# A fused hybrid layer on one core: inputs laid out before the launch, x transposed in memory, its squares summed by VectorE

## The chip, the cores and the metric

One core of a Trainium2 chip runs the whole program. The metric is the device time of one execution in microseconds (us). It has a TensorE (PE) for matrix products, a VectorE (DVE), a ScalarE (ACT), a GpSimd engine (POOL) and a SyncE (SP), whose queue only starts transfers here; 16 DMA engines move data between device memory and the on-chip memory SBUF. TensorE writes its results to PSUM.

## What is computed

One decoder layer over 256 tokens of 2048 features, in float32. The input is normalised, multiplied by one wide matrix, mixed by three groups of heads (retention, gated DeltaNet, block attention), gated, and multiplied by an output matrix:

```python
def rms_norm(x, w):
    return x * lax.rsqrt(jnp.mean(x * x, axis=-1, keepdims=True) + 1e-6) * w

def hybrid_layer(x, norm_w, w_in, ...):
    h = rms_norm(x, norm_w)
    proj = jnp.einsum('btd,de->bte', h, w_in)        # 256 x 2048 by 2048 x 8204
    # 4 retention heads, 6 DeltaNet heads (convolution, L2 norm, gates ga and gb,
    # triangular solve per chunk), 6 attention heads; each times SiLU of its gate
    y = jnp.concatenate([y_ret, y_gdn, y_moba], axis=-1)
    return x + jnp.einsum('bte,ed->btd', y, w_out)   # 256 x 2048 by 2048 x 2048
```

## The kernel before, in words

The instructions of each engine are written out by hand, each engine with its own program, and semaphores order them. The two projections are cut into 160 weight tiles of 128 x 1024 numbers. Tile n is loaded in two transfers of 256 KB into one of 8 buffers `w_raw` (`load`, L396); ScalarE rounds it to a shorter format, `w_hi` (`high_part`, L485, one of 4 buffers); VectorE takes the rest, `w_lo` (`low_part`, L366); TensorE multiplies with both. The activations are split the same way into `hT[:, k, 0]` (high) and `hT[:, k, 1]` (low), for 16 feature blocks k. A tile is used up when TensorE has run its 8 "units", each one 512-column product with `w_hi` and one 256-column product with `w_lo`. The positions of all other work are counted in units: `advance(u)` on ScalarE and VectorE emits the high and low parts that are due before unit u, and `stream(u)` on TensorE emits units up to u. A tile's low part is emitted 2.5 tiles ahead of its use (`LEAD`, `LOW_AT`).

The first group of products (tiles 0 to 7, units 0 to 63) makes the first four columns of blocks of the DeltaNet heads, and the program is special there. x arrives by rows (`x_sb`, tokens on the partitions) in five pieces (`load_piece`). TensorE transposes each pair of feature blocks into PSUM (`x_block`, L1598, by `all_x_blocks`), a tile or two ahead of their use. ScalarE multiplies by the norm's weight and rounds to the high part (`x_high`), VectorE makes the low part from the same PSUM block (L1048), and GpSimd adds both to a whole float32 block (`whole`, L871), which the small products for the gates need (`ab_products`, L1686). The norm's weights come by rows too and are transposed by TensorE (L1649), the other parameters likewise (L1695). The squares of x are summed per token from the rows, half by ScalarE (L557), half by VectorE (L1034).

The scale 1/rms of each token does not go into hT but is applied afterwards: GpSimd raises the mean square to the power -0.5 (`power`), TensorE spreads it over all partitions (L1679), VectorE copies it to `rb` (L1065), and the first projections are multiplied by `rb` (L1074, L1076). From there on VectorE's program is: two additions and two products for the first two sections (L1072, L1074), the gate rows (L1076), then the convolutions of the heads (L1092) and the gates' short chain, with a low part L369 between them whenever one is due.

SyncE's queue issues x's pieces and the weight tiles in one order; from tile 8 on it waits for the low part of tile n - 8.

Of the kernel before, what the change touches and what calls it, by code (L numbers as in the profile page):

```python
# [19 lines left out]
F32 = mybir.dt.float32  # L20
F32R = mybir.dt.float32r
ALU = mybir.AluOpType
# [3 lines left out]
P = 128  # L26
# [35 lines left out]
LOW_AT = 4  # L62

# [11 lines left out]
K_DECAY = K_LEVEL + (LEVELS - 3) * QUART  # L75
K_DIST = K_DECAY + RET * P
K_FIRST_T = K_DIST + 3 * P
K_STACK = K_FIRST_T + QUART
K_KDEC = K_STACK + QUART
K_QDEC = K_KDEC + RET  # L80
K_SUM = K_QDEC + RET
K_COLS = K_SUM + 2 * GDN

# [7 lines left out]
R_ROWS = R_K + 1  # L91

# [43 lines left out]
def layer(nc, x, norm_w, w_in, conv_w, a_log, dt_bias, ret_norm_w, gdn_norm_w, q_norm_w, k_norm_w, w_out,  # L136
          table, out):
    ctx = ExitStack()
    with ctx:
# [12 lines left out]
        bias = sb("bias", [P, 2, GDN])  # L152
        sb("pad", [P, QUART // 2])
# [8 lines left out]
        prow = sb("prow", [R_ROWS, P])  # L162
        pcol = sb("pcol", [P, R_ROWS])
# [33 lines left out]
        x_sb = big[:, :].rearrange("p (c n) -> p c n", c=C)  # L197

        abT = vT[:, 0, :]
        junk_a, junk_v = kq[:, :].rearrange("p h c k t -> p (h c k t)"), sq[:, :].rearrange("p h c k t -> p (h c k t)")  # L200
        def first_bank(k):

            return (mx[0], mx[2], mx[1], mx[3])[k] if k < 4 else mx[k // 2 % 4]
# [66 lines left out]
        def section(g, s):  # L270

            return g % 3, s % 2, 2 * (g // 3) + s // 2

# [17 lines left out]

        def tile_at(n):

            if n < HEADS * TPH:
                return n // TPH, n % TPH
            g, q = OUT_TILES[n - HEADS * TPH]
            return HEADS + g, q
# [67 lines left out]

        def low_part(eng, n):  # L366
# [9 lines left out]
        X_PIECES = [(0, 2), (2, 4), (4, 8), (8, 12), (12, 16)]  # L376
        X_LANDED = [16 * C] + [16] * (len(X_PIECES) - 1)
        SQUARES_AT = {3: 1, 4: 2, 5: 3}

        def load_piece(eng, i):  # L380

            piece = slice(X_PIECES[i][0] * P, X_PIECES[i][1] * P)
            if i:
                eng.dma_start(x_sb[:, :, piece], x[0, :, piece].rearrange("(c p) n -> p c n", p=P)).then_inc(S(f"x_in{i}"), 16)
                return
            for c in range(C):
                eng.dma_start(x_sb[:, c, piece], x[0, c * P:(c + 1) * P, piece]).then_inc(S(f"x_in{i}"), 16)
# [5 lines left out]
        def _(sp):  # L393
            load_piece(sp, 0)

            def load(n):  # L396
                group, q = tile_at(n)
                rows = slice(q * TK * P, (q + 1) * TK * P)
                if n >= NRAW:
                    wait_lo(sp, n - NRAW)  # L400
                dst = w_raw[:, n % NRAW, :].rearrange("p (k n) -> p k n", k=TK)
                if group < HEADS:
                    kind, j = PAIRS[group // 2]
                    heads = {"gdn": GDN, "ret": RET, "moba": MOBA}[kind]
                    first_col = {"gdn": GDN_COL, "ret": RET_COL, "moba": MOBA_COL}[kind]
                    h = 2 * j + group % 2
                    if group == 0:
                        done = [S(f"w_first{n}"), S(f"w_in{n}")] if n < 2 else [S(f"w_in{n % NRAW}")] * TK
                        src = w_in[0, rows, GDN_COL:GDN_COL + 2 * GDN * P].rearrange("(k p) (i c) -> p k i c", p=P, i=2)[:, :, :, 0:2 * P]
                        dst = dst.rearrange("p k (i c) -> p k i c", i=2)  # L410
                        for k in range(TK):
# [1548 lines left out]
```

## Time and profile before

| | us |
|---|---|
| median of 3 runs (510.35 to 510.66) | 510.56 |
| the profiled execution | 510.59 |
| its span, first to last instruction | 508.8 |
| TensorE busy | 503.6 (99%) |
| VectorE busy | 338.8 (67%) |
| ScalarE busy | 279.0 (55%) |
| GpSimd busy | 169.8 (33%) |

The profiled execution took 1.8 us more than its span. TensorE is busy through nearly all of the span. The other engines' shares are means over the program; VectorE's is far above its mean in the first 80 us. Each matmul's end is modelled, so a busy TensorE may still hold a short wait; the weight loads (PEld) show such waits better.

### The profile page before, as it was taken

Reading aid. Unit: us, or ns where it says so; the run is one execution under the profiler, and the core shown is the slowest. Engines: PE = TensorE matmul, PEld = TensorE weight load, DVE = VectorE, ACT = ScalarE, POOL = GpSimd, SP = SyncE. Lnnn points to the kernel's source line nnn. Section 1 sums busy time; section 2 is a strip of 40 time slices with the busy share of each in tenths; the row PEclk is TensorE's granted clock in tenths of the full one; section 3 lists DMA queues with packets and bytes.
Section 4 is the critical chain, followed back from the end, with each engine's and each line's share of the span. In section 5 each row is a group of like instructions: output and inputs, shape, how many; then the busy total and the mean of one; then the engine's idle time right before and its main releaser. Section 6 shows DMA issues by size and latency. Waiting matters only on the chain.

```text
span 508.8 us, 8943 instructions
## 1 busy us (share of the span) xinstructions
PE 503.6 (99%) x3442; PEld 424.1 (83%) x3442; DVE 338.8 (67%) x506; ACT 279.0 (55%) x464; POOL 169.8 (33%) x230
## 2 busy tenths in 40 slices
PE   8999999999999999999999999999999999999997
PEld 6888888888888888888888888888888888888885
DVE  5989998889766876564467455755567566646551
ACT  5776756764347676564537354664556456344340
POOL 5763245445122312134054115506050614230000
PEclk9999999999999999999999999999999999999999
DMA  8997666565654556473975676777775557757711
GB/s 280 346 323 200 166 162 169 159 174 144 190 132 122 132 158 158 134 197 69 292 196 145 167 222 164 201 196 190 193 187 168 166 172 232 221 185 222 260 43 41
DMA packets 154988, 92.61 MB, mean 182 GB/s; under 512 B 15971, under 2 KB 143938, under 8 KB 154946
## 3 DMA queue, kind: packets, MB, share of 16 engines
q1 hardware_dynamic: 151456, 89.86, 62.8%
q10 hardware_dynamic: 3490, 2.18, 1.5%
q8 instruction: 27, 0.44, 0.3%
q14 instruction: 15, 0.12, 0.1%
HBM read 89.00 MB, written 2.10 MB: 179 GB/s over the span
## 4 chain that ended last, share of the span: by engine, by line
PE 99%; POOL 0%; DVE 0%; DVEq 0%; issue 0%; POOLq 0%
PE pj L1574 20%; PE pj L1577 20%; PE pj L1576 20%; PE pj L1552 14%; PE pj L1553 7%; PE pj L1630 3%; PE pj L1639 2%; PE mx L1734 1%; PE pj L1549 1%; PE mx L1787 1%; PE mx L1769 1%; PE mx L1601 1%; PE pj L1647 1%; PE mx L1845 1%; PE mx L1907 1%; PE pj L1548 1%
## 5 line engine op out<-in xcount | busy, mean ns | idle before, releaser
L369 DVE TENSOR_TENSOR w_lo<-w_raw,w_hi 128x1024 fp32r<-128x1024 f32 x160 | 200.7, 1262 | 78.2 <-ACT w_hi L489 77.3
L489 ACT ACTIVATE w_hi<-w_raw 128x1024 fp32r<-128x1024 f32 x158 | 166.1, 1057 | 121.0 <-PE pj L1577 103.7
L1574 PE MATMUL pj<-w_hi,hT 128*128 128x512 f32 x320 | 126.5, 395 | 0.0
L1576 PE MATMUL pj<-w_hi,hT 128*128 128x512 f32 x320 | 126.1, 394 | 0.0
L1577 PE MATMUL pj<-w_lo,hT 128*128 128x512 f32 x320 | 124.7, 390 | 0.0
L1552 PE MATMUL pj<-hT,w_hi 128*128 128x512 f32 x300 | 109.0, 403 | 0.0
L1553 PE MATMUL pj<-hT,w_lo 128*128 128x256 f32 x300 | 84.1, 280 | 0.0
L1577 PEld LDWEIGHTS pj<-w_lo,hT 128*128 128x128 f32 x320 | 60.1, 188 | 12.2
L1574 PEld LDWEIGHTS pj<-w_hi,hT 128*128 128x128 f32 x320 | 60.1, 188 | 12.1
L1576 PEld LDWEIGHTS pj<-w_hi,hT 128*128 128x128 f32 x320 | 60.2, 188 | 11.5
L1552 PEld LDWEIGHTS pj<-hT,w_hi 128*128 128x128 f32 x300 | 56.3, 188 | 13.2 <-DVE w_lo L369 0.6
L927 POOL COPY mT<-mT 32x128 f32<-32x128 f32 x80 | 40.5, 506 | 60.1 <-issue 45.7
L1553 PEld LDWEIGHTS pj<-hT,w_lo 128*128 128x128 f32 x300 | 56.6, 189 | 0.7
L858 POOL TENSOR_TENSOR sm<-sm,cst 128x4 f32<-128x4 f32 (+2 forms) x12 | 15.8, 1314 | 111.8 <-DVE sm L1417 39.3
L1574 PE MATMUL pj<-w_hi,yT 128*128 128x512 f32 x128 | 50.3, 393 | 0.0
L1577 PE MATMUL pj<-w_lo,yT 128*128 128x512 f32 x128 | 49.8, 389 | 0.0
L1576 PE MATMUL pj<-w_hi,yT 128*128 128x512 f32 x128 | 49.8, 389 | 0.0
L897 POOL TENSOR_TENSOR ev<-ev 128x256 f32<-128x256 f32 x22 | 23.7, 1078 | 67.2 <-ACT ev L504 67.0
L1092 DVE SCALAR_TENSOR_TENSOR big<-raw,pcol,big 128x256 f32<-128x256 f32 x54 | 33.8, 627 | 3.2 <-ACT big L527 1.9
L927 POOL COPY kq<-mT 32x128 f32<-32x128 f32 x56 | 32.0, 572 | 11.2 <-DVE mT L1380 8.0
L1577 PEld LDWEIGHTS pj<-w_lo,yT 128*128 128x128 f32 x128 | 24.0, 188 | 5.0
L1576 PEld LDWEIGHTS pj<-w_hi,yT 128*128 128x128 f32 x128 | 24.0, 188 | 4.9
(239 smaller groups left out, 541.2 us busy)
## 6 DMA issues: line engine op xcount, KB each, us to landing
w_raw<-in_w_in_dram SPq DMA_DIRECT2D x256, 256.0 KB, 3.4
w_raw<-in_w_out_dram SPq DMA_DIRECT2D x64, 256.0 KB, 4.1
big<-in_x_dram SPq DMA_DIRECT2D x9, 256.0 KB, 5.3
out_dram<-sq ACTq DMA_DIRECT2D x7, 256.0 KB, 5.8
big<-in_x_dram SPq DMA_DIRECT2D x3, 512.0 KB, 7.1
cst<-table_dram SPq DMA_DIRECT2D x1, 682.0 KB, 9.3
kq<-vr SPq DMA_DIRECT2D x32, 16.0 KB, 1.8
kq<-mT SPq DMA_DIRECT2D x24, 16.0 KB, 1.9
```

The lines of the kernel that those rows point to most:

```text
L369: eng.tensor_tensor(w_lo[:, n % NSPLIT, :], w_raw[:, n % NRAW, :], w_hi[:, n % NSPLIT, :].bitcast(F32), ALU.subtract).then_inc(S("lo"), 1)
L489: act.activation(w_hi[:, n % NSPLIT, :], w_raw[:, n % NRAW, :], ACT.Copy).then_inc(S("hi_done"), 1)
L858: return pool.tensor_tensor(sm[:, dst:dst + n], sm[:, src:src + n], cst[:, K_POW:K_POW + n], ALU.pow)
L897: pool.tensor_tensor(ev[:, n % 2, 0:T], ev[:, n % 2, 0:T], ev[:, n % 2, T:2 * T], ALU.add).then_inc(S("halves"), 1)
L927: ins = pool.tensor_copy(dst[i:i + QUART, :, a:a + QUART], src[a:a + QUART, :, i:i + QUART])
L1092: ins = dve.scalar_tensor_tensor(dst, raw_of(j, h, i, slice(k, k + T)), tap, dst, ALU.mult, ALU.add)
L1552: pe.matmul(pj[s][:, :], high, hT[:, kc].rearrange("p a t -> p (a t)"), start=first, stop=False)
L1553: ins = pe.matmul(pj[s][:, 0:T], low, hT[:, kc, 0, :], start=False, stop=False)
L1574: ins = pe.matmul(bank[:, :], src[:, kc, 0, tok], hi[:, k, :], start=first, stop=False)
L1576: pe.matmul(bank[:, :], src[:, kc, 1, tok], hi[:, k, :], start=False, stop=False)
L1577: ins = pe.matmul(bank[:, :], src[:, kc, 0, tok], lo[:, k, :], start=False, stop=last)
L1630: pe.matmul(pj[s][:, cols], block_of(hi, 0, s, k), hT[:, TK * t + k].rearrange("p a t -> p (a t)")[:, cols], start=t == 0 and a == 0, stop ...
```

## The change

The host part of the program now passes the same numbers in another layout, and the kernel reads these:

- x transposed, feature-major, with the 16 columns of the norm's weight in front. It lands in the place of the whole blocks (`home`), in six pieces; `whole_pair` names two neighbouring blocks. (x by rows is still an input for the sum at the end.)
- the weights cut into the 160 tiles, each 128 x 1024 contiguous: one transfer of 512 KB for each, two of 256 KB for the first three (`HALVED`). All parameters as columns (`cols`); the gates' weights apart.
- `x_high` and `x_low` read x from SBUF. All 32 transposes of x and the two of parameters are gone, and so are the four filling ones (`keep_busy`) and GpSimd's 16 additions.
- GpSimd multiplies the gates' weights by the norm's weight, once.
- Squares: ScalarE squares 8 pairs of blocks (128 x 512) into `big`, VectorE adds the eight (`add_squares`) and the two halves of the sum (`total_squares`), and TensorE sums over the partitions with two one-column products in the middle of tile 7. The power and the spreading over partitions now follow the gates' products.
- In tiles 0 to 2 the high and low products alternate by half tile, and VectorE makes the low part in halves.

```diff
+        def x_squared(b):
+            return big[:, b * 2 * T:(b + 1) * 2 * T]
+        def half_low_part(eng, n, k):
+            cols = slice(k * 512, (k + 1) * 512)
+            eng.wait_ge(S(("hi_first", "hi_done")[k]), n + 1)
+            eng.tensor_tensor(w_lo[:, n, cols], w_raw[:, n, cols], w_hi[:, n, cols].bitcast(F32), ALU.subtract)...
-        X_PIECES = [(0, 2), (2, 4), (4, 8), (8, 12), (12, 16)]
+        X_PIECES = [(0, 2), (2, 4), (4, 6), (6, 8), (8, 12), (12, 16)]
+        SQUARES_AT = {1: (0,), 2: (1,), 3: (2,), 4: (3, 4), 5: (5,), 6: (6,), 7: (7,)}
...
+                sp.dma_start(w_raw[:, n % NRAW, :], tiles[n]).then_inc(S(f"w_in{n % NRAW}"), 16)
...
+            def square(b):
+                act.activation(x_squared(b), whole_pair(b), ACT.Square).then_inc(S("squared"), 1)
             def x_high(k):
-                act.activation(hT[:, k, 0, :], first_bank(k)[:, k % 2 * T:(k % 2 + 1) * T], ACT.Copy,
-                               scale=pcol[:, R_NORM + k:R_NORM + k + 1]).then_inc(S("h_hi"), 1)
+                x_landed(act, k)
+                act.activation(hT[:, k, 0, :], whole(k), ACT.Copy, scale=norm_cols[:, k:k + 1])...
...
-            for n in range(KC):
-                pool.tensor_tensor(whole(n), hT[:, n, 0, :].bitcast(F32), hT[:, n, 1, :].bitcast(F32), ALU.add)...
+            pool.tensor_tensor(wab[:, :, 0:AB], wab_in, pcol[:, R_NORM:R_CONV].unsqueeze(2).broadcast_to([P, KC, AB]),
+                               ALU.mult).then_inc(S("pool_step"), 1)
+            pool.wait_ge(S("norm_step"), 10)
+            power(6, 10, 2).then_inc(S("pool_step"), 1)
...
+            def x_low(k):
+                dve.wait_ge(S("h_hi"), k if k else 1)
+                dve.scalar_tensor_tensor(hT[:, k, 1, :], whole(k), norm_cols[:, k:k + 1],
+                                         hT[:, k, 0, :].bitcast(F32), ALU.mult, ALU.subtract)...
+            def add_squares(b):
+                dve.wait_ge(S("squared"), b + 1)
+                dve.wait_ge(S("norm_step"), b)
+                dve.tensor_tensor(x_squared(0), x_squared(0), x_squared(b), ALU.add)...
...
+                x_low(2 * b)
+                x_low(2 * b + 1)
+                advance(UPT * (b - LEAD) + LOW_AT + 1)
+                add_squares(b - 2)
+            add_squares(6)
+            add_squares(7)
+            total_squares()
+            advance(UPT * (KC // 2 - LEAD) + LOW_AT + 1)
+            dve.wait_ge(S("norm_psum"), 1)
+            dve.tensor_scalar(sm[:, 10:12], mx[3][:, 0:C], 1.0 / D, EPS, ALU.mult, ALU.add)...
             dve.wait_ge(S("norm_psum"), 2)
             dve.tensor_copy(rb[:, :], mx[1][:, 0:T]).then_inc(S("rb_done"), 1)
...
+                first_group_high(t, range(TK))
                 if t == TPH - 1:
-                    pe.wait_ge(S("rstd_done"), 1)
+                    pe.wait_ge(S("norm_step"), 9)
                     for c in range(C):
-                        ins = pe.transpose(mx[1][:, c * P:(c + 1) * P], sm[:, 6 + c:7 + c].broadcast_to([P, P]), ident)
-                    ins.then_inc(S("rb_psum"), 1)
+                        ins = pe.matmul(mx[3][:, c:c + 1], x_squared(7)[:, c * P:(c + 1) * P], er[:, 0, 0:1], ...)
...
+            pe.wait_ge(S("pool_step"), 1)
             ab_products().then_inc(S("abt_psum"), 1)
+            pe.wait_ge(S("pool_step"), 2)
+            for c in range(C):
+                ins = pe.transpose(mx[1][:, c * P:(c + 1) * P], sm[:, 6 + c:7 + c].broadcast_to([P, P]), ident)
+            ins.then_inc(S("norm_psum"), 1)
```

On TensorE, the end of the first group before (L1601 transposes x, L1630 and L1639 are high and low products, L1679 spreads 1/rms, L1695 transposes parameters, L1690 is the gates):

```order
L1630 MATMUL pj<-hT,w_hi 128x512 x8
L1639 MATMUL pj<-hT,w_lo 128x256 x8
L1601 MATMUL mx<-cst,big 128x128 x4
L1630 MATMUL pj<-hT,w_hi 128x512 x8
L1639 MATMUL pj<-hT,w_lo 128x256 x8
L1630 MATMUL pj<-hT,w_hi 128x512 x8
L1679 MATMUL mx<-cst,sm 128x128 x2
L1639 MATMUL pj<-hT,w_lo 128x256 x8
L1695 MATMUL mx<-cst,prow 128x95
L1690 MATMUL mx<-home,wab 32x256 x16
L1552 MATMUL pj<-hT,w_hi 128x512
```

and now (L1629 and L1642 are high and low products, L1661 sums the squares, L1670 is the gates, L1678 spreads 1/rms):

```order
L1629 MATMUL pj<-hT,w_hi 128x512 x8
L1642 MATMUL pj<-hT,w_lo 128x256 x8
L1629 MATMUL pj<-hT,w_hi 128x512 x8
L1642 MATMUL pj<-hT,w_lo 128x256 x8
L1629 MATMUL pj<-hT,w_hi 128x512 x8
L1661 MATMUL mx<-er,big 128x1 x2
L1642 MATMUL pj<-hT,w_lo 128x256 x8
L1670 MATMUL mx<-home,wab 32x256 x16
L1678 MATMUL mx<-cst,sm 128x128 x2
L1563 MATMUL pj<-hT,w_hi 128x512
```

The transposes are gone, the sum of squares stands where the spreading stood, and the spreading has moved behind the gates' products.

On VectorE, the same place before (L1048 low part of x, L369 low part of a tile, L1061 and L1063 finish the sum of squares, L1065 copies `rb`, L1068 copies parameters, L1072 and L1074 scale the first sections, L1076 the gates):

```order
L1048 SCALAR_TENSOR_TENSOR hT<-mx,pcol,hT 128x256 x2
L369 TENSOR_TENSOR w_lo<-w_raw,w_hi 128x1024
L1061 TENSOR_REDUCE sm<-sm 128x2
L1063 TENSOR_SCALAR sm<-sm 128x2
L1048 SCALAR_TENSOR_TENSOR hT<-mx,pcol,hT 128x256 x2
L369 TENSOR_TENSOR w_lo<-w_raw,w_hi 128x1024
L1065 COPY rb<-mx 128x256
L369 TENSOR_TENSOR w_lo<-w_raw,w_hi 128x1024
L1068 COPY pcol<-mx 128x79
L1072 TENSOR_TENSOR ev<-ev 128x256
L1074 TENSOR_TENSOR raw<-ev,rb 128x256
```

and now (L1039 low part of x, L418 low part of a tile, L1051 adds squares, L1045 the two halves, L1076 takes the mean, L1079 copies `rb`, L1083 and L1085 scale the first sections):

```order
L1039 SCALAR_TENSOR_TENSOR hT<-home,hT 128x256 x2
L418 TENSOR_TENSOR w_lo<-w_raw,w_hi 128x1024
L1051 TENSOR_TENSOR big<-big 128x512 x3
L1045 TENSOR_TENSOR big<-big 128x256
L418 TENSOR_TENSOR w_lo<-w_raw,w_hi 128x1024
L1076 TENSOR_SCALAR sm<-mx 128x2
L1079 COPY rb<-mx 128x256
L1083 TENSOR_TENSOR ev<-ev 128x256
L1085 TENSOR_TENSOR raw<-ev,rb 128x256
```

The low part of tile 8 now stands ahead of the copy of `rb` instead of behind it, and three additions of squares end the first group.

## Rows read from the trace of the kernel before

**Rows 1.** The chain of waits, 0 to 62 us: start us, us, what.
```profile
4.45 0.68 PE mx L1601 x4
...
5.67 2.37 PE pj L1630 x12
...
24.76 0.96 PE pj L1639 x8
25.72 0.44 PE mx L1601 x4
26.16 1.85 PE pj L1630 x8
...
30.80 0.22 PE mx L1679 x2
...
32.05 1.86 PE mx L1690 x32
...
36.59 0.35 PE mx L1705 x4
```

**Rows 2.** Waits of the weight loads, whole span: total us, times, longest us.
```profile
PEld pj L1552 <- DVE w_lo L369: 0.6, 2, 0.3
```

**Rows 3.** Busy time in one stretch, VectorE alone, then clock, DMA share, GB/s.
```profile
31.00:57.60 26.60, 25.86 (x46) 1.00 0.81 226
```

**Rows 4.** Timeline, 31 to 58 us: start us, us, instructions.
```profile
31.05 0.42 DVE L1065 COPY rb<-mx 128x256 f32<-128x256 f32 x1 [1.66 <-PE mx L1679]
31.39 1.22 DVE L369 TENSOR_TENSOR w_lo<-w_raw,w_hi 128x1024 fp32r<-128x1024 f32 x1
32.53 0.23 DVE L1068 COPY pcol<-mx 128x79 f32<-128x79 f32 x1
32.68 0.41 DVE L1072 TENSOR_TENSOR ev<-ev 128x256 f32<-128x256 f32 x1
...
56.38 1.21 DVE L369 TENSOR_TENSOR w_lo<-w_raw,w_hi 128x1024 fp32r<-128x1024 f32 x1
...
57.65 0.19 PEld L1552 LDWEIGHTS pj<-hT,w_hi 128*128 128x128 f32 x1 [0.28 <-DVE w_lo L369]
```

**Rows 5.** Timeline, 4.8 to 5.4 us: start us, us, instructions.
```profile
4.80 0.63 ACT L495 ACTIVATE w_hi<-w_raw 128x512 fp32r<-128x512 f32 x1 [1.64 <-DMA w_raw<-in_w_in_dram]
```

**Rows 6.** Busy time of each engine in stretches, then clock, DMA share, GB/s.
```profile
2.00:3.00 1.00, 1.00 (x2) 0.34 (x1) 0.00 (x0) 0.99 (x2) 0.48 (x2) 1.00 0.82 241
3.00:4.00 1.00, 1.00 (x3) 0.34 (x1) 0.00 (x0) 0.16 (x1) 0.00 (x0) 1.00 1.00 306
...
5.00:10.00 5.00, 4.90 (x37) 4.27 (x36) 4.54 (x9) 4.06 (x9) 2.84 (x3) 1.00 1.02 333
10.00:15.00 5.00, 5.00 (x34) 4.34 (x32) 4.67 (x6) 3.56 (x7) 4.79 (x5) 1.00 1.08 390
```

**Rows 7.** Groups by shape, ScalarE: busy us, mean ns, idle before.
```profile
L489 ACT ACTIVATE w_hi<-w_raw 128x1024 fp32r<-128x1024 f32 x158 | 166.1, 1057 | 121.0 <-PE pj L1577 103.7 <-PE pj L1553 16.6
L557 ACT ACTIVATE kq<-big 128x512 f32<-128x512 f32 x4 | 2.5, 628 | 0.0
L781 ACT ACTIVATE yT<-mT,sm 128x256 fp32r<-128x256 f32 x4 | 1.8, 501 | 7.8 <-POOL mT L927 7.8
```

**Rows 8.** Single lines: duration ns min/median/max, first and last start.
```profile
L1048 DVE SCALAR_TENSOR_TENSOR hT<-mx,pcol,hT x16: 467/474/485, 5.6 to 27.8; 128x256 fp32r<-128x256 f32 x16
L1370 DVE SCALAR_TENSOR_TENSOR yT<-mT,sm,yT x4: 479/482/485, 268.0 to 314.7; 128x256 fp32r<-128x256 f32 x4
L1034 DVE SCALAR_TENSOR_TENSOR sq<-big x4: 1221/1222/1226, 8.0 to 23.3; 128x512 f32<-128x512 f32 x4
L369 DVE TENSOR_TENSOR w_lo<-w_raw,w_hi x160: 1183/1226/1767, 6.8 to 495.3; 128x1024 fp32r<-128x1024 f32 x160
L1015 DVE TENSOR_TENSOR sq<-pj,big x7: 681/684/692, 458.4 to 504.4; 128x512 f32<-128x512 f32 x7
L871 POOL TENSOR_TENSOR home<-hT x16: 736/1207/1819, 6.1 to 30.0; 128x256 f32<-128x256 f32 x16
```

More of the change, by code:

```diff
@@ L62 @@
 LOW_AT = 4
+HALVED = 3
 LEVELS = 7
@@ L133, in constants, with tile_at, section, weight_tiles @@
     return t.astype(np.float32)
-def layer(nc, x, norm_w, w_in, conv_w, a_log, dt_bias, ret_norm_w, gdn_norm_w, q_norm_w, k_norm_w, w_out,
-          table, out):
+def tile_at(n):
+    if n < HEADS * TPH:
+        return n // TPH, n % TPH
+    g, q = OUT_TILES[n - HEADS * TPH]
+    return HEADS + g, q
+def section(g, s):
+    return g % 3, s % 2, 2 * (g // 3) + s // 2
+def weight_tiles(w_in, w_out):
+    tiles = np.empty((TILES, P, TK * 512), np.float32)
+    for n in range(TILES):
+        group, q = tile_at(n)
+        rows = slice(q * TK * P, (q + 1) * TK * P)
+        if group >= HEADS:
+            g = group - HEADS
+            tile = w_out[0, rows, g * 512:(g + 1) * 512].reshape(TK, P, 512)
+        elif group == 0:
+            tile = w_in[0, rows, GDN_COL:GDN_COL + 2 * GDN * P].reshape(TK, P, 2, GDN * P)[:, :, :, 0:2 * P]
+        elif group < GDN:
+            p, h, i = section(group, q // 2)
+            at = GDN_COL + (i * GDN + 2 * p + h) * P
+            tile = w_in[0, q % 2 * UPT * P:(q % 2 + 1) * UPT * P, at:at + P].reshape(UPT, P, P)
+        else:
+            kind, j = PAIRS[group // 2]
+            heads, col = {"ret": (RET, RET_COL), "moba": (MOBA, MOBA_COL)}[kind]
+            h = 2 * j + group % 2
+            tile = w_in[0, rows, col:col + 4 * heads * P].reshape(TK, P, 4, heads * P)[:, :, :, h * P:(h + 1) * P]
+        tiles[n] = np.moveaxis(tile, 0, 1).reshape(P, TK * 512)
+    return tiles
+def columns(norm_w, conv_w, a_log, dt_bias, ret_norm_w, gdn_norm_w, q_norm_w, k_norm_w):
+    per_row = [a.reshape(-1, P).T for a in (norm_w, conv_w, ret_norm_w, gdn_norm_w, q_norm_w, k_norm_w)]
+    per_head = [np.broadcast_to(a.reshape(1, GDN), (P, GDN)) for a in (a_log, dt_bias)]
+    return np.ascontiguousarray(np.concatenate(per_row + per_head, axis=1))
+def layer(nc, x, turned_x, tiles, gate_w, cols, table, out):
     ctx = ExitStack()
@@ L393, in _ @@
         def _(sp):
-            load_piece(sp, 0)
             def load(n):
-                group, q = tile_at(n)
-                rows = slice(q * TK * P, (q + 1) * TK * P)
+                if n < HALVED:
+                    for k, done in enumerate((f"w_first{n}", f"w_in{n}")):
+                        if n == k == 1:
+                            load_piece(sp, 1)
+                        cols = slice(k * 512, (k + 1) * 512)
+                        sp.dma_start(w_raw[:, n, cols], tiles[n, :, cols]).then_inc(S(done), 16)
+                    return
@@ L594, in _ @@
                 else:
                     advance(UPT * (b - LEAD + 1))
-                if b in SQUARES_AT:
-                    square_sum(SQUARES_AT[b])
-                if b in (2, 3, 4, 5):
-                    load_params(b - 2)
+                for i in SQUARES_AT.get(b, ()):
+                    square(i)
             advance(64)
-            act.wait_ge(S("bias_in"), 2 * 16)
+            act.wait_ge(S("cols_in"), 16)
             act.activation(sm[:, 16:16 + GDN], bias[:, 0, :], ACT.Exp).then_inc(S("expa_done"), 1)
```

311 lines of the change are left out of this document (114 added, 197 removed).

## The prediction

> **What bounds the kernel now.** I read the page's busy times first (TensorE 99%), then the chain of waits, then who waits for whom, then VectorE's timeline. The chain is TensorE from end to end: in the first 62 us it goes without a gap from one product or transpose to the next [rows 1]. So an instruction that TensorE loses should shorten the program by its time. But the view of waits holds one short entry that says otherwise: twice a weight load waited for VectorE's low part, 0.3 us each [rows 2]. One of these is at 57.65 us, where tile 16 begins [rows 4]: L369 made that tile's low part from 56.38 to 57.59, and TensorE started right behind it. And VectorE has no room before that point: from 31.0 to 57.6 us it is busy 25.86 of 26.60 us, the rest being hops between instructions that depend on each other [rows 3]. That stretch begins at the copy of `rb` at 31.05 us, for which VectorE had waited 1.66 us [rows 4]. So there are two bounds: TensorE up to about 33 us, and VectorE's fixed row of instructions from the copy of `rb` to tile 16. What TensorE gains before 33 us is kept only as far as VectorE's row also begins earlier. After tile 16 TensorE is the bound again, and carries whatever shift it has there to the end.
>
> **The change on TensorE.** Seven batches of transposes of x behind the first product go, 0.44 us each in the chain [rows 1]: 3.1 us. The parameters' transpose (L1695) is about 0.1. Two one-column products come in; the nearest row is L1705, four records for two products, 0.35 us [rows 1], and I take 0.3. Start: the first product waits for the rounded half tile. It landed at 4.80 us [rows 5], issued behind two transfers of x; now behind one, and ScalarE makes one block of x ahead of it, so I expect the first product near 5.3 instead of 5.67: 0.4. Together 3.3 us, if nobody is late for it. Now who is late.
>
> **The change on VectorE and ScalarE, first group.** Low part of x: 0.474 us from PSUM; the same instruction with both tensors in SBUF is L1370, 0.482 [rows 8]: no change. Squares: before, four of 1.222 us; now seven additions of 128x512, 0.684 each by L1015, and one of 128x256, about 0.42 as L1065 or L1072 [rows 4, 8]. That is 4.9 before and 5.2 now: nothing gained, but they have moved: three additions and the halves now stand behind the last low part of x. GpSimd's 16 additions go. While they ran, L369 took up to 1.767 us against 1.183 at least [rows 8]; I take 1.22 for it in the first group. ScalarE: 0.50 for a high part of x from SBUF (L781), 1.06 for a tile, 0.63 for a square [rows 7]; that is 2.7 us per tile and less than TensorE's 0.96 + 1.85 = 2.81 [rows 1].
> Consecutive instructions on VectorE start 0.08 us closer than their duration (L369 starts at 31.39, takes 1.22, the next starts at 32.53 [rows 4]).
>
> VectorE's row, worked out. The data: up to the first half of tile 2, queues carry 2.16 MB (x's first 270 KB, parameters 55 KB, seven pieces of 262 KB). Before, the engines moved 241 GB/s in the third microsecond, 306 in the fourth, 333 from 5 to 10 us and 390 from 10 to 15 [rows 6]; with 2 KB rows instead of 1 KB I take 360. From 2.05 us on that gives 8.05; the first half tile landed 0.7 to 0.8 us later than the bytes ahead of it explain, so 8.85. ScalarE then rounds that half (0.6), squares a pair (0.55) and makes block 4 (0.5): 10.5 us. From there VectorE has left, by spacing: 12 low parts of x at 0.40 (4.8), 2 half tiles at 0.60 (1.2), 5 tiles at 1.13 (5.7), 5 additions at 0.60 (3.0), 2 that wait for the one before at 0.73 (1.5), and 0.45 for the halves: 16.7 us. I add 0.9 for ScalarE, which it follows closely in tiles 2 and 3, and 0.35 for the one time that GpSimd's product for the gates (192 columns; L871's 256 take 0.736 alone) runs into it. The squares are complete at 28.45 us.
>
> TensorE would be there at 27.1 (5.3, eight times 2.81 less the last low half of 0.95, and 0.3 of early waits), so it stands still 1.4 us in the middle of tile 7. Then: hop 0.1, sums 0.3, low half 0.95, gates 1.86, spreading 0.22 [rows 1]: 31.9 us. GpSimd's power is ready before that. TensorE's stream of units so starts at 31.9 instead of 33.9: 2 us earlier. VectorE copies `rb` (hop 0.05, 0.42 and 0.04 until the next may start) and begins L1072's successor at 32.4. Before, it began at 32.68 [rows 4], since the low part of tile 8 and the parameter copy stood between; these are gone from this place. The row behind it is the same, instruction by instruction, so tile 16's low part comes 0.25 us earlier than before, and TensorE, 2 us early at 33 us, gives 1.7 us of that back in waits at tiles 9, 14 and 16. No later wait in the views has less room, as the rest of both programs shifts alike.
>
> Sum: 510.59 (profiled execution, 0.03 above the median of the runs) less 0.25: **510.3 us**.
>
> Unknown costs, from both sides. Data rate in the first 10 us: 300 GB/s as before at its slowest, or 400; by the same steps VectorE's row begins 1.9 us later or 0.6 earlier than my 360 gives. An addition of squares in place: 0.684, or up to 0.73 each if it collides: +0.3. The collision with GpSimd: 0 to 0.6. The chain of low parts behind 33 us holds five pairs of GpSimd instructions that stretch VectorE's; they can fall luckier or worse by 0.5. Loads of 512 KB instead of two of 256: the buffers are 8 deep, ScalarE sat waiting for TensorE and not for data (L489: 103.7 us [rows 7]), so I cost it at nothing in the stream.
>
> The Trainium skill speaks against the low parts of x: "Vector Engine (DVE) Microarchitecture Reference", section "Points that are easy to get wrong", says that a scalar_tensor_tensor with two SBUF sources that are not bf16 runs at half throughput. The trace says both: L1034, which has two SBUF sources and also accumulates, takes 1.222 us for 512 columns; L1370, two SBUF sources and no accumulation, takes 0.482 for 256, the full rate. By the rows the rule does not hold without the accumulator; by the rule it would be rival 3.
>
> **The rivals.**
> 1. *VectorE does not hold it back.* If VectorE's row between 31 and 58 us is shorter now (fewer collisions with GpSimd, data at 400 GB/s and no collision before 28 us), TensorE keeps 1.2 to 2.3 us: 508.3 to 509.4. For it: the limit is a single point, tile 16, and only 0.3 us of waiting show it. Against: a stretch that is 97% busy in a fixed order.
> 2. *The data come late.* At 300 GB/s the half tile that I have at 8.85 lands at 10.0, and the later pieces add to it: the copy of `rb` ends at 34.1 and not 32.4, so VectorE is 1.5 us late at tile 16: 512.0. It decides from about 350 GB/s down (no gain), and is slower by 0.2% from 315 down. For it: 306 GB/s in the fourth microsecond with all DMA engines busy. Against: rows of 1 KB then, of 2 KB now.
> 3. *Low parts of x at half rate.* 0.69 us instead of 0.48, from L1034's 1.222 for 512 columns: 12 after the start of the full row, 2.5 us, less some 0.9 that now is waiting: 1.6 us later, 511.9. For it one kind of row, against it another.
> 4. *TensorE's sum works differently:* the two squares' sums wait longer than their row, 0.6 instead of 0.3, or VectorE's last four additions collide. That stays within 0.5 us of the forecast.
>
> **How the numbers follow.** 0.2% is 1.02 us; about what a measurement of this kernel can tell from no change. My forecast, VectorE takes the gain back, has 0.56 (with the fourth): of it 0.49 within 0.2%, 0.04 faster, 0.03 slower. Rival 1 has 0.22, nearly all faster. Rival 2 has 0.13 (0.10 slower), rival 3 0.07 (0.06 slower); 0.02 for what I have not seen. That makes faster 0.26, the same 0.53, slower 0.21. Range 508.8 to 512.1: it leaves out the better half of rival 1 and what lies beyond rivals 2 and 3; the forecast's own range is 509.6 to 511.2.
>
> **What the new profile would show.** Right: the first product near 5.3 us; TensorE idle 1 to 2 us inside tile 7, released by the addition L1045; VectorE idle before the copy L1079, released by the spreading; L1083 first at 32.0 to 32.8; waits of weight loads for L418 of 1.5 us or more in all between 33 and 58 us; L1039 at 0.48. Wrong: no such waits and a stream that stays 2 us early (rival 1); ScalarE waiting for transfers in tiles 2 to 5 (rival 2); L1039 at 0.69 (rival 3). If TensorE does not stop in tile 7, my row of VectorE is too long; if it stops for 3 us, too short.

## The result

| median us (lowest to highest) | before | changed |
|---|---|---|
| first timing | 510.48 (510.33 to 510.87, 8 runs) | 511.70 (511.38 to 512.81, 8 runs) |
| the profiled execution, span | 510.59, 508.8 | 511.47, 509.7 |

The ratio is 1.0024 (95% interval 1.0015 to 1.0034). The changed kernel is 1.2 us slower, where 510.3 was forecast; the time lies inside the range (508.8 to 512.1), but on the side that had 0.21, and above the forecast's own 509.6 to 511.2. Two later timings, each on one chip, gave ratios of 1.0030 (1.0020 to 1.0040) and 1.0021 (1.0012 to 1.0030).

The place where TensorE first waits for VectorE, from the timeline of the changed kernel (columns: start, duration, instructions, and in brackets the idle time before them with what ended it):

```profile
28.24 0.43 DVE L1045 TENSOR_TENSOR big<-big 128x256 f32<-128x256 f32 x1
28.58 1.22 DVE L418 TENSOR_TENSOR w_lo<-w_raw,w_hi 128x1024 fp32r<-128x1024 f32 x1
...
28.72 0.61 PE L1661 MATMUL mx<-er,big 128*128 128x1 f32 x4 [0.81 <-DVE big L1045]
29.16 1.01 PEld L1642 LDWEIGHTS pj<-hT,w_lo 128*128 128x128 f32 x8
...
29.72 0.15 DVE L1076 TENSOR_SCALAR sm<-mx 128x2 f32<-128x2 f32 x1
...
30.31 1.94 PE L1670 MATMUL mx<-home,wab 128*32 128x256 f32 x32
32.17 0.19 PEld L1678 LDWEIGHTS mx<-cst,sm 128*128 128x128 f32 x2 [0.41 <-issue]
32.17 0.43 PE L1678 MATMUL mx<-cst,sm 128*128 128x128 f32 x2
...
32.64 0.42 DVE L1079 COPY rb<-mx 128x256 f32<-128x256 f32 x1 [2.77 <-PE mx L1678]
...
33.10 0.43 DVE L1083 TENSOR_TENSOR ev<-ev 128x256 f32<-128x256 f32 x1
```

This answers to [rows 4]. The squares are complete at 28.67 us (28.24 + 0.43), and TensorE, idle for 0.81 us, goes on at once. The spreading L1678 comes last, so the copy of `rb` starts at 32.64, after VectorE has been idle for 2.77 us, and L1083 stands at 33.10, where its predecessor L1072 stood at 32.68 [rows 4]. The waits that follow, from the timeline of the weight loads at tiles 9, 14 and 16, and then the same wait in the view of waits (total, times, longest):

```profile
36.62 0.19 PEld L1563 LDWEIGHTS pj<-hT,w_hi 128*128 128x128 f32 x1 [0.71 <-DVE w_lo L418]
...
51.22 0.19 PEld L1563 LDWEIGHTS pj<-hT,w_hi 128*128 128x128 f32 x1 [0.62 <-DVE w_lo L418]
...
58.05 0.19 PEld L1563 LDWEIGHTS pj<-hT,w_hi 128*128 128x128 f32 x1 [0.58 <-DVE w_lo L418]
```
```profile
PEld pj L1563 <- DVE w_lo L418: 2.2, 4, 0.7
```

Before, the same wait summed to 0.6 us [rows 2]. Tile 16's first weight load stood at 57.65 [rows 4], now at 58.05. I set the first product of each unit against the same one of before (columns: start before; shift of the changed kernel, us):

```
unit 64 (stream begins)  33.85  -1.49
unit 72 (tile 9)         37.22  -0.59
unit 112 (tile 14)       51.21  +0.01
unit 128 (tile 16)       57.65  +0.41
unit 168                 75.09  +0.22
unit 304                130.54  +0.84
end of the projections'
last group, from        483.10  +0.99
```

So TensorE has 1.5 us in hand at the start of the stream and has lost 1.9 by tile 16. That is the forecast's mechanism with a larger loss: 1.7 was forecast. Of the 2.2 us in the view of waits 1.9 stand in these three waits. A second loss, which was not forecast, lies between units 296 and 304, in the triangular solve. The chain of waits of the changed kernel there (start, duration, what):

```profile
127.71 0.48 PE mx L1768 x38
128.19 0.36 issue
128.55 0.69 PE mx L1768 x46
```

In the middle of a run of equal small products TensorE stops for 0.36 us, and "issue" says that nothing the profile shows held it. From unit 296 to 304 0.62 us are lost in all. The profile before has no gap over 0.1 us behind its start.

### The profile page after: what moved, and what is told of

The parts are those of the page before. It is cut to its first block, busy times and chain, and to the rows that moved or that the text cites. A ratio compares the mean times of both kernels' runs of the same rounds, so it can differ in the third digit from the quotient of the medians.

```text
span 509.7 us, 8693 instructions
## 1 busy us (share of the span) xinstructions
PE 500.8 (98%) x3408; PEld 420.6 (83%) x3408; DVE 336.5 (66%) x506; ACT 280.7 (55%) x465; POOL 151.8 (30%) x215
## 4 chain that ended last, share of the span: by engine, by line
PE 89%; DVE 7%; DMA 1%; issue 1%; ACT 1%; SPq 1%; DVEq 0%
PE pj L1588 20%; PE pj L1587 20%; PE pj L1585 20%; PE pj L1563 11%; PE pj L1564 6%; DVE w_lo L418 3%; DVE big L1103 2%; DMA w_raw<-in_w_tiles_dram 1%; PE mx L1715 1%; DVE big L1051 1%; PE mx L1768 1%; PE mx L1750 1%; PE pj L1560 1%; PE mx L1826 1%; PE mx L1888 1%
## 5 line engine op out<-in xcount | busy, mean ns | idle before, releaser
L418 DVE TENSOR_TENSOR w_lo<-w_raw,w_hi 128x1024 fp32r<-128x1024 f32 x157 | 195.0, 1251 | 78.1 <-ACT w_hi L520 77.7
L535 ACT ACTIVATE ev<-pj 128x512 f32<-128x512 f32 x24 | 14.1, 594 | 26.3 <-PE pj L1560 20.5
```

Of the source, the lines that this page charges most:

```text
L535: act.activation(ev[:, n % 2, :], pj[s][:, :], ACT.Copy).then_inc(S("ev_done"), 1)
```

## The experiments

Each was timed beside the kernel before on the same chip. Before had 511.0 us beside the changed kernel again (first time), spreading first, halves and only the weights; 510.8 beside halves and spreading first, short additions, filler and halves in the solve; 510.75 beside quarters, filler with halves and spreading first, the changed kernel a third time and before again; 510.96 beside the last three (no data in the solve, and the second timings of spreading first and of halves and spreading first). Shifts are against the first profile of before. Where nothing else is said, an edit is made on the changed kernel.

**The changed kernel again**, twice, unaltered.

> The changed kernel unaltered, once more, beside the kernel before. In its first trace TensorE entered the stream of units 1.5 us early, lost 1.9 us in three waits for VectorE's low parts (tiles 9, 14 and 16) and stood 0.41 us late at tile 16, and lost another 0.62 us at 128 us in the solve, in a pause of 0.36 us that no semaphore explains. Theory A (VectorE's row began 0.42 us late, and the pause is an accident of this execution): the median is again near 511.5, the lateness at tile 16 again 0.4, the pause is gone or elsewhere. Theory B (the pause belongs to this program): it is at the same instruction again, 0.3 to 0.7 us.

> The changed kernel unaltered, on the same chip as these. 511.5 to 512.5, TensorE +0.4 to +0.9 us at tile 16 and a pause of 0.3 to 0.9 us in the solve, as twice before. No pause in this profile would say that it is not bound to this program.

Measured: 512.48 (511.54 to 513.14, 7 runs), ratio 1.0030 (1.0020 to 1.0040); and 511.89 (511.13 to 512.83, 11 runs), 1.0021 (1.0012 to 1.0030). Shifts at tile 16: +0.92 and +0.29. In the solve (units 296 to 312) they lose 1.33 and 0.23 us. So both losses recur, and both vary from one execution to the next. What varies at tile 16 stands in TensorE's first tiles. Its first eight products, in the first profile of the changed kernel and then in the second:

```profile
5.52 1.22 PE L1629 MATMUL pj<-hT,w_hi 128*128 128x256 f32 x8 [1.28 <-ACT w_hi L526]
```
```profile
5.58 2.08 PE L1629 MATMUL pj<-hT,w_hi 128*128 128x256 f32 x8 [1.34 <-ACT w_hi L526]
...
27.47 2.01 PE L1629 MATMUL pj<-hT,w_hi 128*128 128x512 f32 x8
29.32 0.50 PE L1661 MATMUL mx<-er,big 128*128 128x1 f32 x4
```

In the second, a product of 256 columns starts every 0.21 us instead of every 0.12, and a weight load takes 330 ns instead of 188, up to 10.3 us; the view gives a granted clock of 1.00, the upper of its two levels, for both, so it does not name the reason. TensorE then comes to the sums at 29.32, after the squares (28.62), and does not stand idle in tile 7. Of the fourteen profiles with the new inputs for x, nine begin so slowly (until 8.4 to 10.8 us) and five do not. The two of before and that of only the weights, which have transposes and filling products right ahead of the first product, do not either. The changed kernel has nothing there: TensorE is idle for 1.3 us ahead of its first product. Whether this makes the slow start is not shown; with 17 small products in that place (the filler below) it was slow once and not slow once.

VectorE's row is rigid in spite of it. In the six profiles with the spreading behind the gates' products (these three, halves, halves in the solve, filler) the copy of `rb` starts between 32.52 and 33.14, and tile 16's shift is each time that start less 32.21 to 32.23.

**Spreading first.** The place of the spreading is put back to where it was before, ahead of the gates' products.

```
-            pe.wait_ge(S("pool_step"), 1)
-            ab_products().then_inc(S("abt_psum"), 1)
             pe.wait_ge(S("pool_step"), 2)
             ... (the spreading)
             ins.then_inc(S("norm_psum"), 1)
+            ab_products().then_inc(S("abt_psum"), 1)
```

> The changed kernel with the spreading of 1/rms (two transposes) put ahead of the gates' sixteen products instead of behind them; same instructions. My theory, that VectorE's row from the copy of rb to tile 16 is the limit: the copy starts at 31.2 instead of 32.6 us, TensorE waits 0.3 us for the power and loses that, tile 16 starts 1.0 to 1.4 us earlier than in the changed kernel, and the time falls by as much, to 510.2 to 510.7. The rival, that the loss sits in the loads or in the fetching of instructions and not in that row: no change or 0.3 us slower, 511.7 to 512.0.

> Spreading first with 512 KB loads, for the second time: 510.6 to 510.9, -0.1 to +0.1 against before; TensorE -0.3 us or less at tile 16 by an execution that starts at 6.0 us, -1.1 by one that starts at 5.5; a loss of 0.2 to 1.1 us in the solve.

Measured: 510.89 (11 runs), ratio 0.9996 (0.9988 to 1.0005); again 510.36 (12 runs), 0.9998 (0.9984 to 1.0011). The timeline of the first, at the same place:

```profile
29.83 0.50 PE L1661 MATMUL mx<-er,big 128*128 128x1 f32 x4
...
31.46 0.40 PE L1677 MATMUL mx<-cst,sm 128*128 128x128 f32 x2
...
31.79 1.93 PE L1670 MATMUL mx<-home,wab 128*32 128x256 f32 x32
31.90 0.42 DVE L1079 COPY rb<-mx 128x256 f32<-128x256 f32 x1 [1.37 <-PE mx L1677]
32.36 0.42 DVE L1083 TENSOR_TENSOR ev<-ev 128x256 f32<-128x256 f32 x1
```

The copy starts 0.74 us earlier (31.90 instead of 32.64), although this execution was late at its start (a slow one, until 10.8 us: sums at 29.83 instead of 28.72, with the squares complete at 28.32). No weight load waits for a low part any more: the waits at tiles 9, 14 and 16 are gone, and tile 16 is at -0.31 and -0.56. The change had moved the spreading behind 1.86 us of products [rows 1], and VectorE's row began later for it. In the timing that had both, this swap alone is 1.6 us faster than the changed kernel (512.48 and 510.89). The two profiled executions, both with a slow start, differ by the same 1.6 us: 1.2 of it at tile 16, 0.3 in the solve.

**Halves.** Tiles from 3 on come as two transfers of 256 KB, in rows of 2 KB instead of 4.

```
-   sp.dma_start(w_raw[:, n % NRAW, :], tiles[n])
+   for k in range(TK):
+       cols = slice(k * 512, (k + 1) * 512)
+       sp.dma_start(w_raw[:, n % NRAW, cols], tiles[n, :, cols])
```

> The changed kernel with every weight tile from tile 3 on loaded as two transfers of 256 KB (packets of 2 KB) instead of one of 512 KB (packets of 4 KB). If the longer packets hold up what TensorE fetches (its instructions come in packets of 16 KB over the same engines), the pause at 128 us goes: 0.4 to 0.6 us faster than the changed kernel, near 511.1. If the pause comes from where the fetches fall in the program, or by chance, no change: 511.5 to 511.7. Tile 16 late by 0.4 as before in both.

Measured: 511.71 (11 runs), 1.0018 (1.0009 to 1.0027); +0.43 at tile 16, no pause in the solve. Beside the changed kernel in the same timing (512.48) it is 0.8 us faster. This looked as if the size of the packets made the pauses. The next runs were made to test that.

**Halves and spreading first**, both edits together, twice.

> The changed kernel with both single edits together: tiles from 3 on loaded as two transfers of 256 KB (2 KB rows), and the spreading of 1/rms ahead of the gates' products. If the two losses are separate, they add: against before, the spreading alone stood at 0.9996 although its profile had a pause of 0.58 us in the solve, and the halves alone took the pause away. So I expect TensorE at -0.3 to -0.5 us at tile 16, no idle time of TensorE over 0.1 us in the solve (123 to 155 us), and 510.2 to 510.6 us, ratio 0.999 to 1.0. Rival (the pause belongs to this order of instructions and not to the size of the packets): a pause of 0.3 us or more in the solve as in all three profiles with the 512 KB loads, and 510.8 to 511.2, as with the spreading alone.

> Halves and spreading first, for the second time and beside the 512 KB loads. If halving the loads is worth something of its own (0.7 us between medians in one pair, at changed kernel and halves), it is 0.3 to 0.7 us faster than the spreading alone: 510.1 to 510.4. If it is worth nothing, as the 1.1 us pause with quarters suggests, the two are within 0.2 us of each other.

Measured: 510.08 (509.47 to 511.03, 11 runs), 0.9987 (0.9978 to 0.9995); again 510.23 (509.44 to 512.14, 12 runs), 0.9990 (0.9980 to 1.0001). This is the best version: 0.7 us under before's median both times (the second interval just reaches 1), where the changed kernel is 1.1 to 1.5 above. But the first profile loses 0.34 us in the solve, with packets of 2 KB. And beside the spreading alone in one timing it gains 0.13 us between medians, where halves alone had gained 0.8 beside the changed kernel: halving has no clear worth.

**Only the weights laid out**, the rest as before.

> The kernel before with one part of the change: the weights laid out tile by tile, one transfer of 512 KB each (two for tiles 0 and 1). x, its transposes, its squares and the parameters stay as before. If the layout of the weights costs nothing by itself: 510.4 to 510.6, TensorE's chain as before, DMA busy share lower. If packets of 4 KB hold up the fetching of instructions: pauses in TensorE's solve and 0.3 to 0.8 us slower.

Measured: 513.52 (6 runs), 1.0058 (1.0046 to 1.0071), a miss for my expectation. The time is lost before the stream begins: unit 64 is at +2.45. ScalarE's timeline shows where; first this kernel, then before:

```profile
14.24 5.56 ACTq L565 DMA_DIRECT2D prow<-in_conv_w_dram  x1
...
16.32 0.20 ACT L556 ACTIVATION_READ_ACCUMULATOR kq<-big 128x1 f32 x1
19.85 0.47 ACT L575 ACTIVATE hT<-mx,pcol 128x256 fp32r<-128x256 f32 x1 [3.33 <-issue]
```
```profile
13.35 2.98 ACTq L566 DMA_DIRECT2D prow<-in_conv_w_dram  x1
```

ScalarE starts a small parameter load itself, and the start takes it 5.56 us beside 512 KB loads, against 2.98 before; its next high part of x begins at 19.85, behind 3.33 us of idle time, where before had it at 16.47, and TensorE later waits 1.1 us for a high part of the weights. The changed kernel has all parameters in `cols` and none of these starts on ScalarE, but no run has the two layouts without the rest, so that they pay together is not shown. This profile also loses 0.45 us in the solve, with TensorE's instructions as before; more on that under what is open.

**Short additions.** On halves and spreading first: the seven additions of squares cover 8 of 512 columns, so the sum of squares is incomplete.

```
-   dve.tensor_tensor(x_squared(0), x_squared(0), x_squared(b), ALU.add)
+   dve.tensor_tensor(x_squared(0)[:, 0:8], x_squared(0)[:, 0:8], x_squared(b)[:, 0:8], ALU.add)
```

> As the kernel with halves and spreading first, but the seven additions of squares are made over 8 of their 512 columns (this part of the computation is left out, all waits stay). It takes about 7 x 0.6 = 4.2 us from VectorE's row ahead of the first group's end. If VectorE's row is what holds TensorE in tile 7 (0.81 us idle there after the change), that idle time goes, and all behind it comes 0.8 us earlier, since the copy of rb follows the spreading at once: 0.7 to 0.9 us less than the kernel with halves and spreading first, some 509.6. Rival (TensorE's idle time in tile 7 only stands in for waits that come anyway, at tile 16 or for data): less than 0.3 us gained.

Measured: 509.65 (508.0 to 509.81, 6 runs), 0.9970 (0.9959 to 0.9982). TensorE's waits ahead of the stream, first with the additions whole (halves and spreading first, view of waits: total, times, longest), then the same place with short additions (timeline):

```profile
PE mx L1663 <- DVE big L1047: 0.8, 1, 0.8
PE mx L1679 <- POOL sm L868: 0.4, 1, 0.4
```
```profile
28.02 0.50 PE L1663 MATMUL mx<-er,big 128*128 128x1 f32 x4
28.39 1.19 PE L1644 MATMUL pj<-hT,w_lo 128*128 128x256 f32 x8
29.65 0.40 PE L1679 MATMUL mx<-cst,sm 128*128 128x128 f32 x2
```

Both waits of the products are gone (a weight load still waits 0.25 us for the power), and tile 16 goes from -0.79 to -2.11, by 1.32 us: the 1.2 of the two waits and an earlier start. So VectorE's row did hold TensorE in tile 7. The two profiled executions differ by 0.83 us (510.14 and 509.31), since this one lost 0.82 us in the solve and the other 0.34. The medians differ by 0.43, less than the 0.7 to 0.9 that I expected; the solve may have taken the rest there too, but medians cannot show it.

**Quarters, fillers, and halves in the solve only.** Quarters: spreading first, four transfers of 128 KB per tile, rows of 1 KB. Filler: 17 products of 32x32 ahead of the first tile, as many instructions as the change took away. Halves in the solve: 256 KB transfers for tiles 42 to 59 alone.

```
+   for _ in range(17):
+       pe.matmul(pj[3][0:QUART, 0:QUART], er[0:QUART, 0, 0:QUART], er[0:QUART, 0, 0:QUART], ...)
```

> The changed kernel, with only the tiles 42 to 59, whose loads are issued from about 112 to 165 us, as two transfers of 256 KB; the others stay at 512 KB. Theory (TensorE's instructions come late in the solve because their fetches stand behind data packets of 4 KB): no pause over 0.1 us in the solve, and the same time as with all tiles halved (511.7 median there, -0.3 to -0.8 us against the unaltered changed kernel, of which it had 512.5 when run side by side). Rival A (the pause comes from how the TensorE program lies against the boundaries of its fetches, or from chance): the pause stays, 0.3 to 0.8 us. Rival B (the loss of the 512 KB loads is spread over the whole stream): the pause goes, but the time is that of the unaltered one.

> The changed kernel with 17 products of 32x32 (68 instructions of TensorE, as many as the transposes and what went with them had) ahead of everything, during the wait for the first data. It puts all later instructions of TensorE at the places in its program that they had before. Rival to the theory of packets (the pause in the solve comes with where TensorE's blocks of instructions begin, and these moved by some 70 instructions): no pause in the solve with 512 KB loads. Theory of packets: the pause of 0.3 to 0.8 us stays, perhaps at other instructions; time as the unaltered changed kernel within 0.3 us plus at most 0.3 for the start.

> Halves and spreading first, and the 17 filler products of 32x32 ahead of everything. The halves alone do not take the pause away for good (0.3 us with halves and spreading first, 0.6 us with short additions), while the filler with 512 KB loads had none. Theory now: the pause comes where a block of TensorE's instructions is used the moment it is fetched, and which instructions stand there depends on the count ahead of them; 68 more put the edges elsewhere. Then no pause here, and the filler's own cost is 0.4 us at the start, given back by TensorE's idle 0.8 us in tile 7: 509.7 to 510.1, against 510.1 without the filler. Rival (chance, any kernel with early TensorE): a pause of 0.3 us or more in the solve.

> Spreading first, and tiles from 3 on as four transfers of 128 KB, rows of 1 KB. Theory of packets (an instruction fetch stands behind data packets, and the larger these are, the later it is): no pause, and executions spread less than with 2 or 4 KB: 509.6 to 510.0. Rival (the position of the blocks, whatever the packets): pause of 0.3 us or more as with halves at these positions, 510.0 to 510.4.

Measured: halves in the solve 511.65 (11 runs), 1.0017 (1.0008 to 1.0026), no pause in its profile; filler 511.47 (11 runs), 1.0012 (1.0004 to 1.0021), no pause; filler with halves and spreading first 510.32 (11 runs), 0.9989 (0.9980 to 0.9998), 0.5 us lost in the solve; quarters 510.45 (11 runs), 0.9989 (0.9980 to 0.9998), 1.07 us lost behind later packets, the largest part of it here (chain of waits):

```profile
139.34 0.83 PE mx L1752 x59
140.18 0.41 issue
140.59 0.32 PE mx L1752 x11
```

I had expected no pause with quarters and none with the filler and halves, and one with the filler alone; all three were wrong. Packets of 1 KB have the pauses too, and so has the program with the filler. Neither theory stands: the size of the packets does not make them, nor does the count of instructions ahead.

**Before again.**

> The kernel before, unaltered, for a second profile. What I want from it is the time at which TensorE's instruction packets are fetched in the solve. If fetches that come late are a property of the new inputs, this second profile shows no pause of TensorE over 0.1 us in the solve either, as the first. If they are chance in every kernel, it may show one of 0.3 to 0.8 us.

Measured: 510.61. Its profile loses 0.04 us between units 296 and 312.

**No data in the solve.** What all profiles have in common is told by the records of the DMA queues. TensorE's instructions arrive in packets of 16 KB (queue 8; 27 packets with 0.44 MB in the whole program), one about every 4 us in the solve, and nearly every one starts only when a weight tile has kept the DMA engines full for 1.5 to 2 us. Two neighbouring stretches of spreading first, from the view of DMA queues (busy share in 40 slices; queue: packets, MB, share of 16 engines):

```profile
DMA  6957948959939159559399691953975555583765
...
q1 hardware_dynamic: 195, 0.71, 87.9%
```
```profile
q1 hardware_dynamic: 37, 0.11, 25.1%
q8 instruction: 1, 0.02, 5.5%
```

The first is 128 to 130.3 us: 88% busy, no instruction packet. The second is 130.3 to 131.4, the end of the burst: the packet starts at 130.34 and lands at 131.30. TensorE stops at 132.05 and goes on at 132.63, 1.33 us behind the landing. In all ten pauses over 0.1 us in the solve this distance is 1.26 to 1.60 us. What fills it the profile does not show, so the tie between packet and pause rests on the next run and on the table behind it. The experiment keeps all instructions and waits of spreading first, but the loads of tiles 42 to 59 bring 8 of their 1024 columns; the weights of these tiles are left out.

```
+   cols = slice(0, 8 if 42 <= n < 60 else TK * 512)
-   sp.dma_start(w_raw[:, n % NRAW, :], tiles[n])
+   sp.dma_start(w_raw[:, n % NRAW, cols], tiles[n, :, cols])
```

> As the kernel with spreading first, but the loads of tiles 42 to 59 (issued from about 112 to 165 us) bring 8 of their 1024 columns, so that the weights of these tiles are left out; all waits and instructions stay. Theory now: TensorE's pauses in the solve are fetches of its instructions that stand behind a burst of weight data. Without the bursts the instruction packets start some 1 to 2 us earlier against the program's place, none is late, and no pause is left: 0.3 to 0.8 us less than the spreading alone on this chip. Rival (the fetches are late by themselves): pauses as before, sum 0.2 to 1.1 us, and no gain.

Measured: 509.73 (509.07 to 510.01, 9 runs), 0.9975 (0.9965 to 0.9984), beside 510.36 (509.43 to 513.22) for spreading first with its data: 0.63 us, and 0.3 to 0.8 was expected. The busy times in 122 to 135 us, with the data (first execution) and then without (busy time of TensorE, weight loads, VectorE, ScalarE, GpSimd; clock, DMA share, GB/s):

```profile
122.00:135.00 13.00, 12.41 (x338) 10.35 (x338) 10.73 (x15) 4.15 (x5) 4.60 (x4) 1.00 0.64 205
```
```profile
122.00:135.00 13.00, 13.00 (x400) 10.88 (x403) 10.05 (x14) 4.65 (x6) 4.62 (x4) 1.00 0.05 6
```

TensorE's 0.59 us of idle time are gone with the data, at full clock in both. Then I took, from all profiles in which TensorE's instructions stand at the same places (the filler ones left out), when two of the packets have landed, on a clock that TensorE's own shift is taken out of, and what TensorE lost behind each:

```
                              packet 1    lost   packet 2    lost
no data in the solve            125.38    0.00     129.83    0.00
halves                          125.99    0.00     130.34    0.00
short additions                 126.05    0.00     131.61    0.82
halves + spreading, 2nd         126.06    0.01     131.13    0.05
quarters                        126.09    0.00     130.60    0.00
halves in the solve             126.18    0.01     130.64    0.02
changed kernel, 3rd             126.35    0.00     130.97    0.23
spreading first, 2nd            126.37    0.00     131.15    0.48
spreading first                 126.44    0.25     131.59    0.76
changed kernel, 2nd             126.57    0.27     131.58    1.06
halves + spreading              126.72    0.34     130.67    0.00
changed kernel                  127.07    0.62     130.84    0.00
```

Up to 126.37 us packet 1 costs nothing, from 126.44 on more the later it lands; for packet 2 the edge is near 130.9 (of those behind it, one landed at 131.13 and lost only 0.05). The packet's landing explains the loss, and the run without data lands both earlier than all others, by 0.6 and 0.5 us at least. So the pauses in the solve are TensorE waiting for its own instructions, and these wait for weight data. (Leaving the data out also takes their writes into SBUF away; the table is what speaks for the packets.)

## Why the prediction was wrong

*The first product, near 5.3 us.* 5.52, and 5.35 to 6.05 in other executions; ScalarE had its half tile at 4.83, as before [rows 5], behind the block of x. The sum has nothing for the slow start that nine of fourteen profiles show. It costs nothing where TensorE would wait for the squares anyway, and 0.5 us in the second profile of the changed kernel (the copy of `rb` at 33.14 instead of 32.64).

*The data, 8.85 us for tile 2's first half.* ScalarE waited for it until 9.63. From 5 to 10 us the DMA engines moved 343 GB/s, not 360, but 412 from 10 to 15:

```profile
5.00:10.00 5.00, 4.48 (x33) 4.29 (x34) 3.46 (x7) 3.53 (x7) 0.00 (x0) 1.00 1.01 343
10.00:15.00 5.00, 4.65 (x28) 3.93 (x27) 3.79 (x8) 5.00 (x11) 0.00 (x0) 1.00 1.03 412
```

So the data were 0.8 us late, and 343 is below the 350 GB/s from which rival 2 would leave no gain. But VectorE's row caught up: squares complete at 28.67, forecast 28.45. Rival 2's delay came in part, but the squares were 0.2 us late and not 1.7.

*Low parts of x and additions.* As taken, 0.48 and 0.68:

```profile
L1039 DVE SCALAR_TENSOR_TENSOR hT<-home,hT x15: 467/479/736, 4.9 to 24.4; 128x256 fp32r<-128x256 f32 x15
...
L1051 DVE TENSOR_TENSOR big<-big x7: 673/683/693, 15.6 to 27.5; 128x512 f32<-128x512 f32 x7
```

Rival 3 is refuted. The rule of the Trainium skill ("Vector Engine (DVE) Microarchitecture Reference", "Points that are easy to get wrong") that two such SBUF sources halve the throughput does not hold for this form.

*TensorE idle 1.4 us in tile 7.* 0.81, since it came there at 27.91 and not at 27.1.

*The sum behind the squares, 31.9 for the end of the spreading.* This is the first step that failed. From start to start, the two one-column products took 0.47 (28.72 to 29.19) and not 0.3, the low half 1.12 (to 30.31) and not 0.95, the gates' products 1.86 as taken, the spreading 0.43 from its start to its end and not 0.22, and the squares were 0.22 late: 0.7 us together. The 0.22 was a piece of the chain of waits, which leaves out what overlaps with the product ahead; in the timeline of before the same two transposes take 0.38:

```profile
30.64 0.38 PE L1679 MATMUL mx<-cst,sm 128*128 128x128 f32 x2
```

L1083 stood at 33.10, not 32.4. Each of the three was sized by a row that stood among other neighbours. By the forecast's own rule, VectorE's row is rigid to tile 16, this turns its -0.25 into +0.42, and +0.41 was measured. The rule was right (six profiles agree with it within 0.02 us), and spreading first shows it from the other side.

It was written in the prediction that the spreading now follows 1.86 us of gates' products. The sum contained them, but I did not ask what the order itself cost: put back, it is worth 1.2 us at tile 16 between the two profiles with the same slow start, and 1.6 us in all.

Rival 1 is out, since the waits for L418 came (1.9 us, with 1.5 or more forecast), and rival 4 came in part: the two sums took 0.47, between its 0.6 and the 0.3 of the sum.

*"After tile 16 TensorE is the bound again, and carries whatever shift it has there to the end."* This is the second step that failed. In the solve it loses 0.2 to 1.3 us more in the three profiles of the changed kernel. I costed the new loads "at nothing in the stream" because buffers and ScalarE had room; I did not think of the instruction packets, which use the same DMA engines.

*What is open.* Both profiles of before lose under 0.1 us there, with the same bytes and bursts as full. Only the weights has TensorE's instructions as before has them, and the two kernels with the filler have them within a few of the same places. The same packet 2, on the same clock, in these five profiles:

```
                              packet 2    lost
before, again                   126.93    0.00
before                          129.12    0.00
filler                          129.84    0.01
weights only                    130.69    0.45
filler, halves + spreading      130.93    0.48
```

So the landing decides here too, and before loses nothing because its packet lands at least 1.5 us ahead of the two that cost. Why it lands earlier there is open, and so is whether it does in executions without a profile.

The sum for the changed kernel, over its three profiles: at tile 16 +0.41, +0.92, +0.29; in the solve +0.62, +1.33, +0.23; in all +0.99, +2.19, +0.64 where the last group of the projections ends. The profiled executions themselves took 511.47, 512.71 and 511.13 us, that is +0.88, +2.12 and +0.54 against 510.59; the medians differ by +1.2, +1.5 and +1.1.

## What to carry over

When an edit takes work off the bounding engine, follow the next engine's first fixed point and size every small instruction between the two in the place where it will stand, not by a row from among other neighbours; and look first at the order, since one swap here was worth 1.6 us. A gain before such a point is only lent: 1.5 us in hand at 33 us were gone at 58. And a stretch of many short instructions on the bounding engine has a second supply, its instruction packets, that shares the DMA engines with the data: when two profiles differ by an "issue" gap among equal instructions, look at when these packets started. And before profiles of two kernels are compared far into the program, compare the spacing of their first products: here one execution began at about half the rate of another of the same kernel.

## What the runs showed of the hardware

- A 16 KB instruction packet takes 0.9 to 1.5 us in most cases and starts late behind a burst of data, whether in rows of 1, 2 or 4 KB; TensorE then loses up to 1.06 us behind one packet in the solve, where one lasts some 4 us. It goes on 1.26 to 1.60 us behind the landing.
- In nine of fourteen profiles with the new x TensorE's first tiles ran with 330 ns for a weight load instead of 188, until 8.4 to 10.8 us, while the view gave a granted clock of 1.00.
- The start of one small load (`conv_w`) from ScalarE's own queue took 2.98 and 3.14 us beside 256 KB loads (the two profiles of before) and 5.56 us beside 512 KB loads (one profile); the other starts there took 0.23 to 0.60 us.
- Two products with one moving column each held TensorE for 0.47 us (28.72 to 29.19) behind an idle stretch, and for 0.37 (28.02 to 28.39) without one, in the run with short additions.
- A scalar_tensor_tensor on 256 columns takes 0.474 us with a source in PSUM [rows 8] and 0.479 with all in SBUF.
